# A decoder step with 32 experts: router turned round and woven into the last projection, samples turned ahead of the mask, weights fetched in the order of need from the fourth pair on

## What is computed

```python
def rms_norm(x, g):
    return x * lax.rsqrt(jnp.mean(x * x, axis=-1, keepdims=True) + EPS) * g

def decoder_layer(x, ...):
    y, ... = head_group_mixer(rms_norm(x, g_mix), ...)   # projections, RG-LRU scan, conformer conv
    x = x + y
    x = x + cross_attention(rms_norm(x, g_xa), mem_k, mem_v, w_q, w_o)
    x = x + routed_experts(rms_norm(x, g_moe), moe_w)
    return x, ...

def routed_experts(xf, ...):                      # N tokens x 1024
    logits = xf @ w_router + b_router             # 32 experts
    top_v, top_e = lax.top_k(logits, 4)
    gates = jax.nn.softmax(top_v, axis=-1)
    ...                                           # tokens sorted by expert
    gu = xb @ w_e1[e] + b_e1[e]                   # 1024 -> 2048
    g = jnp.minimum(gu[:, :1024], 7.0)
    u = jnp.clip(gu[:, 1024:], -7.0, 7.0)
    h = (u + 1.0) * (g * jax.nn.sigmoid(1.702 * g))
    rows = h @ w_e2[e] + b_e2[e]                  # 1024 -> 1024
    ...                                           # times gate, summed over the 4 experts of a token
```

## Time and profile before

| | us |
|---|---|
| median of 3 runs | 1257.3 |
| lowest, highest | 1255.49, 1258.81 |
| profiled execution | 1259.0 |
| its span in the trace | 1257.4 |
| PE busy | 1160.8 (92%) |
| DVE busy | 335.7 (27%) |
| ACT busy | 181.5 (14%) |
| first expert matmul | 312.96 |
| last weight byte read | 1223.7 |

### The profile page before, as it was taken

One profiled execution on the slowest core, in us unless ns is written; L12 is line 12 of the kernel. 1 busy time (PEld: TensorE's weight loads), 2 busy tenths in 40 slices (PEclk: granted clock), 3 DMA queues, 4 the chain that ended last, 5 costly groups with the idle time before them and its releaser, 6 DMA issues.

```text
span 1257.4 us, 14280 instructions
## 1 busy us (share of the span) xinstructions
PE 1160.8 (92%) x5512; PEld 567.2 (45%) x5512; DVE 335.7 (27%) x814; ACT 181.5 (14%) x353; POOL 45.6 (4%) x87
## 2 busy tenths in 40 slices
PE   8999999698999999989999898999898999999996
PEld 6887888387343343323333333334233333333332
DVE  3795423615112212021212121212212021212113
ACT  3114213203010110111010101010110111010102
POOL 4000001100000000000000000000000000000000
PEclk9999999798899999999999999999999999999998
DMA  9388434993899999999999999999999999999990
GB/s 301 95 285 283 138 101 135 342 424 126 343 429 427 428 427 428 426 429 428 427 427 429 428 427 429 427 428 427 430 427 427 428 428 428 427 429 428 427 397 35
DMA packets 65575, 457.42 MB, mean 364 GB/s; under 512 B 5491, under 2 KB 34379, under 8 KB 40837
## 3 DMA queue, kind: packets, MB, share of 16 engines
q1 hardware_dynamic: 62576, 452.00, 87.6%
q10 hardware_dynamic: 1117, 3.04, 0.6%
q0 software_dynamic: 1856, 2.02, 0.6%
HBM read 453.71 MB, written 3.81 MB: 364 GB/s over the span
## 4 chain that ended last, share of the span: by engine, by line
PE 54%; DMA 39%; DVE 4%; ACT 1%; issue 1%; ACTq 0%; SPq 0%; POOL 0%; DVEq 0%
DMA ring<-in_w_e 39%; PE ps L1589 21%; PE ps L1307 11%; PE ps L1608 8%; PE ps L1326 3%; PE ps L1556 2%; DVE ring L997 2%; PE ps L1565 2%; PE ps L1510 1%; PE ps L1469 1%; PE ps L1598 1%; PE ps L1254 1%; PE ps L1243 1%; PE ps L1501 1%; PE ps L1248 0%
## 5 line engine op out<-in xcount | busy, mean ns | idle before, releaser
L1589 PE MATMUL ps<-ring,mixed 128*64 128x512 f32 x1536 | 351.8, 607 | 50.4 <-DMA ring<-in_w_e 49.3
L1589 PEld LDWEIGHTS ps<-ring,mixed 128*64 128x64 f32 x1536 | 108.2, 139 | 278.6 <-issue 197.6
L1608 PE MATMUL ps<-ring,mixed 128*64 128x512 f32 x1024 | 230.9, 604 | 0.7 <-issue 0.7
L1147 DVE TENSOR_SCALAR mixed<-ps 128x512 f32<-128x512 f32 x32 | 22.1, 691 | 592.1 <-PE ps L1589 592.1
L1608 PEld LDWEIGHTS ps<-ring,mixed 128*64 128x64 f32 x1024 | 71.9, 139 | 157.9 <-issue 145.8
L721 ACT ACTIVATE mixed<-mixed 128x512 f32<-128x512 f32 x32 | 20.2, 630 | 530.0 <-DVE mixed L1147 530.0
L1565 PEld LDWEIGHTS ps<-mixed 128*128 128x128 f32 x512 | 64.1, 200 | 25.8 <-issue 24.3
L1565 PE MATMUL ps<-mixed 128*128 128x128 f32 x512 | 70.0, 292 | 1.3 <-ACT rstd L703 1.3
L731 ACT ACTIVATE mixed<-ps 64x512 f32<-64x512 f32 x64 | 37.8, 591 | 230.4 <-PE ps L1608 230.0
L1134 DVE SCALAR_TENSOR_TENSOR mixed<-mixed,gates 128x1024 f32<-128x1024 f32 x15 | 19.3, 1285 | 153.2 <-ACT mixed L731 153.2
L1307 PE MATMUL ps<-mixed,ring 128*128 128x264 f32 x256 | 58.9, 393 | 0.3 <-ACT mixed L674 0.3
(11 more groups left out here) (299 smaller groups left out, 775.8 us busy)
## 6 DMA issues: line engine op xcount, KB each, us to landing
ring<-in_w_e SPq DMA_DIRECT2D x160, 2048.0 KB, 23.6
low<-in_w_e SPq DMA_DIRECT2D x15, 2048.0 KB, 25.4
mixed<-in_w_e SPq DMA_DIRECT2D x15, 2048.0 KB, 26.7
ring<-in_w_in SPq DMA_DIRECT2D x8, 1024.0 KB, 15.6
ring<-in_cache_mem_k SPq DMA_DIRECT2D x8, 1024.0 KB, 4.8
ring<-in_cache_mem_v SPq DMA_DIRECT2D x8, 1024.0 KB, 8.3
ring<-in_w_k SPq DMA_DIRECT2D x4, 1024.0 KB, 8.9
ring<-in_w_v SPq DMA_DIRECT2D x4, 1024.0 KB, 12.6
```

What stands on the lines that cost most here:

```text
L1147: dve.tensor_scalar(g1, ps[0][:, :], LIMIT, None, ALU.min).then_inc(S["g_clamped"], 1)
L1589: m = pe.matmul(ps[gu][CAP * i:CAP * i + CAP, :], xeT[:, k, CAP * e2:CAP * e2 + CAP], w[:, D * gu + 512 * i:D * gu + 512 * i + 512], start ...
L1608: m = pe.matmul(ps[3][CAP * i:CAP * i + CAP, :], hTv[:, k % 4, CAP * (k // 4):CAP * (k // 4) + CAP], ring[:, s, D * (k % 2) + 512 * i:D * ...
```

## The change

**Router.** `turn_tokens` and the logits' matmuls go. `project` calls `between_tiles` after each output tile: `turn` transposes the tile before to banks 4 to 6 (three transposes), and `route` adds it to router sums in bank 7 with the operands exchanged, `wr[:, k, :]` stationary and the 264 tokens moving; the squares, made by ScalarE tile by tile, are summed in the same way with ones. Each takes 32 columns of the array, another four for odd k. After the last tile VectorE copies the sums, and three small matmuls with `spread` (two stacked identities and a column of 1/32) give logits and mean square by token. `xnt` now holds the raw tokens; 1/rms goes into the one-hot values and the gain into the copy of the gathered rows (`keep_gathered`: eight copies with scale instead of two; in the first pair VectorE does half of them). The tiles 0 and 1 go through logits and mask ahead of the samples' tile. The samples' own turning (L1664 before) becomes a matmul with a diagonal of 1/rms ahead of the mask, and the gates come after the first gather.

**First and last pair.** The output bias is added for both tiles in the first pair. Half of the samples' early matmuls (`early_samples`) moves from the last up projection to behind `turn_gates`.

**Weights.** From pair 4 (`EARLY_PAIRS`) on the order in SP's queue is rest of 2q, head of 2q+1, rest of 2q+1, head of 2q+2. The late half of `high` waits for `logit_done`.

```diff
-            def two_experts(q, last):
-
-                if last:
-                    rest(2 * q, 2 * q)
-                for s in range(0, HEAD_SLOTS, 2):
-                    fill(2 * q + 1, s, used(2 * q - 1, s + 1))
-                if not last:
-                    rest(2 * q, 2 * q)
-                    for s in range(0, HEAD_SLOTS, 2):
-                        refill(2 * q + 2, s, used(2 * q, s + 1))
+            with sp.Fori(1, EARLY_PAIRS) as q:
+                odd_half(q)
+                rest(2 * q, 2 * q)
+                even_half(q + 1)
                 rest(2 * q + 1, 2 * q + 1)
...
+            with sp.Fori(EARLY_PAIRS, PAIRS - 1) as q:
+                rest(2 * q, 2 * q)
+                odd_half(q)
+                rest(2 * q + 1, 2 * q + 1)
+                even_half(q + 1)
+            rest(NE - 2, NE - 2)
+            odd_half(PAIRS - 1)
+            rest(NE - 1, NE - 1)
...
-            pool.wait_ge(S["xnt_kept"], 6)
+            pool.wait_ge(S["logit_done"], 1)
             pool.memset(acc, 0.0).then_inc(S["acc_zeroed"], 1)
...
+            def turn(k):
+
+                pe.wait_ge(S["res_added"], KD + k + 1)
+                if k == 4:
+                    pe.wait_ge(S["tokr_kept"], 3)
+                for t, (t0, rows) in enumerate(TT):
+                    m = pe.transpose(ps[4 + t][0:rows, P * (k % 4):P * (k % 4) + P], xT[:, k, t0:t0 + rows], ident[:, :])
...
+            def route(k):
+
+                r = NE * (k % 2)
...
+                pe.matmul(ps[7][r:r + NE, 0:TOK], wr[:, k, :], xn[:, k, :], start=(k < 2), stop=(k >= KD - 2))
+                r += 2 * NE
+                m = pe.matmul(ps[7][r:r + NE, 0:TOK], ones[:, 0:NE], squares[:, k, :], start=(k < 2), stop=(k >= KD - 2))
...
+            project("o", "o_done", lambda k: oT[:, k, :], o_free, lambda k: None, after=between_tiles)
...
+            dve.tensor_copy(sums, ps[7][:, 0:TOK]).then_inc(S["sums_kept"], 1)
...
-                                                 rkp[:, t, bass.ds(col, 1)], None, ALU.is_equal)
+                                                 rkp[:, t, bass.ds(col, 1)], trs[:, t:t + 1], ALU.is_equal, ALU.mult)
...
                 if first:
+                    pe.wait_ge(S["gt0_kept"], 1)
                     pe.wait_ge(S["be2_loaded"], 16)
-                    rounds(None, 0)
-                if last:
-                    pe.wait_ge(S["acc_done"], 2 * q)
+                    for t in range(2):
+                        rounds(None, t, PAIR_BANKS[t])
...
                 turn_gates(q)
+                if last:
+                    early_samples(1)
                 turn_h(2 * q + 1)
```

More of the change, by code:

```diff
@@ L196, in build @@
         ysb = part(D)
+        acc = part(D)
         b1q = part(512)
-        acc = part(D)
+        sums = part(TOK)
+        diag = part(NB)
         assert pos[0] <= ATTENTION_W
@@ new lines, in _, with logits @@
+            wide = [P, 3, 4, NE]
+            def logits(tiles):
+                for t in tiles:
+                    rows = TT[t][1]
+                    dve.scalar_tensor_tensor(out=lg[0:rows, t, :], in0=root_of[0:rows, t, 0:NE], scalar=trs[0:rows, t:t + 1],
+                                             in1=brout[0:rows, :], op0=ALU.mult, op1=ALU.add).then_inc(S["lg_ready"], 1)
+                dve.wait_ge(S["lg_ready"], 2 if tiles[0] == 0 else 5)
+                for t in tiles:
+                    dve.max(m8[:, t, :], lg[:, t, :]).then_inc(S["lg_ready"], 1)
+                dve.wait_ge(S["lg_ready"], 4 if tiles[0] == 0 else 6)
@@ new lines, in _ @@
+            logits((0, 1))
+            chosen((0, 1), 0)
+            dve.wait_ge(S["eq_ready"], 1)
+            dve.tensor_reduce(mask[:, 0:2, :], eq[:, 0:2, :, :].rearrange("p t k e -> p t e k"), AX.X, ALU.add).then_inc(S["mask_ready"], 1)
+            logits((2,))
+            dve.tensor_scalar(nv0, m8[:, :, 0], -1.0, None, ALU.mult).then_inc(S["v0_ready"], 1)
+            dve.wait_ge(S["mask_ready"], 1)
+            dve.tensor_scalar(rk[:, 0:2, :], mask[:, 0:2, :], -BIG, BIG, ALU.mult, ALU.add).then_inc(S["rank_chain"], 1)
@@ new lines, in _, with one_hot @@
+            dve.wait_ge(S["rank_chain"], 1)
+            dve.wait_ge(S["rank_done"], 1)
+            dve.tensor_tensor(rkp[:, 0:2, 0:NE], rk[:, 0:2, :], ps[7][:, 0:2 * NE].rearrange("p (t e) -> p t e", t=2),
+                              ALU.add).then_inc(S["rank_chain"], 1)
+            dve.wait_ge(S["rank_chain"], 2)
+            def one_hot(cols):
+                for t in range(2):
+                    for i, col in enumerate(cols):
+                        last = dve.tensor_scalar(sel[:, t, CAP * i:CAP * i + CAP], iota_s[:, :],
+                                                 rkp[:, t, bass.ds(col, 1)], trs[:, t:t + 1], ALU.is_equal, ALU.mult)
+                last.then_inc(S["sel_ready"], 1)
@@ L1165, in _ @@
             swiglu(0)
-            add_round(0, 0)
+            for t in range(2):
+                add_round(0, t, PAIR_BANKS[t])
             next_pair(0, first=True)
@@ L1533, in _ @@
                     lhs = before if i == t else ones
-                    m = pe.matmul(ps[5][:, NE * t:NE * t + NE], lhs[:, :], mask[:, i, :], start=(i == 0), stop=(i == t))
+                    m = pe.matmul(ps[7][:, NE * t:NE * t + NE], lhs[:, :], mask[:, i, :], start=(i == 0), stop=(i == t))
             for i in range(2):
-                m = pe.matmul(ps[5][:, 96:128], ones[:, :], mask[:, i, :], start=(i == 0), stop=(i == 1))
+                m = pe.matmul(ps[7][:, 96:128], ones[:, :], mask[:, i, :], start=(i == 0), stop=(i == 1))
             m.then_inc(S["rank_done"], 1)
-            for j in range(10, 12):
-                turn_tokens(j)
-            pe.wait_ge(S["gate_chain"], 4)
-            for t, (t0, rows) in enumerate(TT):
-                m = pe.transpose(ps[4][0:NE, t0:t0 + rows], gcol[0:rows, t, :], ident[0:rows, 0:rows])
-            m.then_inc(S["gt0_turned"], 1)
             def rounds(q, t, bank=6):
@@ L1612, in down, with early_samples @@
                         m.then_inc(S["freed"], 1)
+            def early_samples(i):
+                cols = slice(512 * i, 512 * i + 512)
+                pe.matmul(ps[LAST_BANKS[2] + i][0:NB, :], gateT[:, SEQ:TOK], be2[0:NE, cols], start=True, stop=False)
+                pe.matmul(ps[LAST_BANKS[2] + i][0:NB, :], pick8[:, :], acc[:, cols], start=False, stop=False)
             def pair(q, first=False, last=False):
@@ L1618, in gather_next @@
                     if k == 3 and not last:
[L1619 to L1620 removed]
+                        pe.wait_ge(S["acc_done"], 2 * q + 2)
                         gather(q + 1, (0,))
```

253 lines of the change are left out of this document (128 added, 125 removed).

## The result

| | before | after |
|---|---|---|
| median, us | 1257.96 (6 runs, 1255.49 to 1259.51) | 1249.45 (6 runs, 1247.85 to 1250.25) |
| profiled execution / its span | 1259.0 / 1257.4 | 1250.25 / 1248.7 |
| start of the output projection | 258.81 | 257.47 |
| end of its last tile | 289.03 | 294.26 |
| first expert matmul | 312.96 | 314.25 |

The ratio is 0.9932, 95% interval 0.9919 to 0.9945: 0.7% faster, 8.5 us, where 16 were forecast. The spans differ by 8.7 us, and the table splits that into three: the experts start 1.3 us later, the stream of weights loses 0.7 us more in the first pair (2.9 for 2.2), and the stretch from the last byte to the end of the last down is 8.5 us instead of 19.2, 10.7 less. So the tail came as forecast, and router and first pair, forecast at -3.1 and -2.0, cost 2.0 us together.

What follows compares the result with a forecast made beforehand. Expert weight transfers at 427 GB/s were taken as the bound. Tail -10.9, first pair -2.0 and router -3.1 sum to -16.0 us, from 1257.3 to 1241.3, stated as 1241.5; the 8-in-10 range was 1237 to 1250.

Steps and rivals of the forecast that it cites:

- Order and tail: End of the kernel: transfers in order of need let the last down projection end earlier, at full clock; -10.9 us.
- rival 4: Expert stream: short waits at nearly every transfer lower TensorE's clock and slow the kernel, 1281 us; chance 0.05.
- rival 1: First pair and tail: TensorE's clock falls at both short holes, giving 1246.7 us; chance 0.15.
- last 14.5 us unchanged: Sign that the forecast holds: the kernel's last 14.5 us stay as they were.
- Rival 3: Tail: it is TensorE's own work and does not shrink with the transfer order; 1246.3 us, chance 0.09.
- First pair: First expert pair: with no idle time left the weight stream no longer runs short; -2.0 us.
- The bound +0.8: First pair: value if the clock falls to 1.2 GHz there too and the longer rounds add time.
- Router ahead of the last tile: Output projection: six turns and six router steps between tiles, 0.80 us each, add +4.8 us, bound +7.4.
- The prediction's sign of being wrong: Output projection: tiles over 4.7 us apart would show the forecast wrong.
- Router behind the last tile: Last projection tile to first expert matmul: 15.6 us instead of 23.9, -8.3 us, bounds -9.6 and -6.9.
- Clearing beside the copy: Router: GpSimd's clearing of the sums' rows blocks VectorE's copy of the sums; +0.4 us.
- rival 2: Router: steps run one by one and the chain behind is slower, router +0.9, 1245.3 us; chance 0.14.

Runs made afterwards that it cites:

- run 1: Changed kernel with the transfers of pairs 4 to 14 put back into the old order; 1252.98 us, ratio 0.9958.
- run 2: Kernel before with only the new order of transfers from pair 4 on; 1251.53 us, ratio 0.9953.
- run 3: Changed kernel with the new order of transfers from the first pair of the loop instead of the fourth; 1256.62 us, ratio 0.9994.
- run 4: Changed kernel with the first pair's bias rounds given 128 rows, 96 of them zeros; 1247.03 us, ratio 0.9916.
- run 9: Changed kernel with router steps taken two at a time behind every second tile, the last two behind the last tile; 1245.85 us, ratio 0.9903.
- run 8: Changed kernel with all eight router steps behind the last projection tile; 1244.70 us, ratio 0.9892.
- run 5: Changed kernel with useless matmuls filling TensorE's holes in the router and the up bias behind the small matmuls; 1251.2 us, ratio 0.9938.
- run 6: Changed kernel with useless matmuls in the router's holes and first-pair bias rounds of 128 rows, 96 of them zeros; 1246.87 us, ratio 0.9915.
- run 10: Changed kernel with all router steps behind the last tile and first-pair bias rounds of 128 rows, 96 of them zeros; 1243.49 us, ratio 0.9880.
- run 11: Kernel of run 10 with useless matmuls only at TensorE's standstills and in the samples' diagonal, up bias behind the ranks; 1246.17 us, ratio 0.9904.
- run 7: Kernel before, with its own router, plus the new transfer order and the first- and last-pair changes; 1248.10 us, ratio 0.9920.

## Why the prediction was right, and where it was wrong

**Order and tail: right** (-10.9 forecast, -10.7 by the traces). The steps hold one by one: in step with the transfers by the last expert, hole 0.63 us, down 7.09 us, no fall of the clock at the short holes (rival 4 falls, and rival 1 for the tail), last 14.5 us unchanged (14.5 and 14.6). Runs 1 and 2 show what the sum did not say, that order and last-pair edits each give more than half of it and overlap: the old order with the new last pair has 12 to 13 us behind the last byte, and the new order with the old last pair 11 to 12, of which it pays 2.5 us for the clock behind its hole. Rival 3 fell with run 2. Run 3 bears out that the first pairs have no stock to spend.

**First pair: wrong** (-2.0 forecast, +0.7 measured). The step that failed is "I take -2.0, for there is no idle time left between up projection and transposes". It took idle time as what the clock fell after. The trace after has none and the clock fell (0.85 in 328.20:334.42, then 0.74); run 4 keeps the same busy time, fills the rows with zeros, and it stays up, as it does in the four other kernels with padded rounds. The bound +0.8, written beside it for this case, was the value.

**Router ahead of the last tile: mis-sized** (+4.8 forecast, +6.6 measured; that the last tile ended at 294.26 where 293.8 was forecast is the earlier start of the projection, not a hit). The term is 6 x 0.80 with 0.36 for a turn and 0.44 for a step. A turn cost 3.89 - 3.56 = 0.33; a step cost 0.76. I had costed the step by its passes, two column groups at a time, and not the break in the stream of tiles: the first pass starts 0.10 us later behind the turn than a tile does (0.42 for 0.32), the second 0.25 behind the first, the second holds the engine 0.32 us until the tile, and the tile behind it takes 3.83 instead of 3.73, which makes the 0.76. And since 32 of the bank's rows alternate between even and odd steps, taking them one at a time left half of the width unused, which run 9 shows. The prediction's sign of being wrong, tiles over 4.7 us apart, was too lax: 4.65 us stayed under it and still cost 1.8 us more than the sum had.

**Router behind the last tile: mis-sized** (-8.3 forecast, -3.9 measured; 15.6 us forecast, 20.0 measured). To the logits it took 4.75 us instead of 4.1; 0.4 of it because the small matmuls waited behind the up bias (296.29 to 297.31) when the sums were already copied (296.91). Logits to mask took 2.46 for 2.4: right. Mask to one-hots took 3.9 for 1.8: the samples' diagonal, said to lie "beside the ranks and the gather", stood in front of the ranks until 302.65 while the mask was there at 301.47, and the ranks took 2.35 us at 1.2 GHz. One-hots to gather took 1.1 for 0.7, the gather 6.48 for 5.45, and the step to the experts 1.3 for 1.1. Most of the 4.4 us is the clock, an estimate from these rows: at full clock the diagonal takes 2.05 us (run 8) and would end before the mask, 1.2 us; the ranks take 1.2 (run 5), 1.1 us less; the gather 1.0 over its forecast; 3.3 together. I took the old gather's mean of 0.71 over into a chain with three rows of small, half-empty matmuls before it. And 1.2 of the 4.4 us is this one execution, since runs 1 and 3 took 18.8 us with the same code.

**Clearing beside the copy: wrong** (+0.4 forecast, 0 measured). The copy of the sums took 0.43 us beside GpSimd's clearing, no more than a residual of the same size:

```profile
296.48 0.43 DVE L1056 COPY mixed<-ps 128x264 f32<-128x264 f32 x1 [1.20 <-PE ps L1560]
```

```profile
296.44 0.95 POOL L516 MEMSET mixed<- 128x1024 f32 x1 [43.71 <-PE ps L1560]
```

The rule of the Trainium skill ("SBUF — State Buffer", section "Who interferes with whom") that the prediction set against its row held: no contention for one input from PSUM. Its other half, that `tensor_scalar` can use both ports and then blocks or is blocked whole, agrees with runs 4, 6, 10 and 11: 1.70 us instead of 0.98.

So of rival 2 ("the router only moves") the direction was right and its bound, +0.9, too mild: the router cost 2.6 us in the trace, and 1.35 by the medians of run 7. The range held the time because it took that rival in, and in part by luck: 1249.45 lies 0.55 us inside its upper end of 1250, where neither the forecast (1241.5, its own range ending at 1246) nor any of rivals 1 to 3 (1245.3 to 1246.7) stood. Only the tail was foreseen as it came.

## What to carry to other kernels

A small step woven into a stream of large matmuls costs its passes and the break it makes, whatever the room beside it: gather such steps until they fill all column groups, or put them behind. When a chain of small operations is shortened, look at the clock it will run at; busy time in the rows does not say that the clock stays up, and filling a hole pays only where the filler ends before the wait does. A gain in a tail has two parts, when the last data comes and what is left to do at which clock, and each can hide the other. Rest no stage on one trace where the clock may fall at another moment: look at a second run with the same code there.

## What the runs showed of the hardware

- TensorE's clock fell from 2.4 to 1.2 GHz with no idle time in the rows: in the first pair (1.00 until 328.20) after 3.7 us of matmuls on 32 rows, and in run 11 right after 8.8 us of mixed small work that had run at 1.00. With zeros in the 96 missing rows it did not fall, at the same busy time, in five kernels of five. No run tried data in their place.
- The moment of the fall differs between executions of the same code (the diagonal took 3.58, 3.15 and 3.23 us in the changed kernel and runs 1 and 3, 2.05 in run 8). What sets it stays open.
- Passes of 264 columns start 0.22 us apart at full clock, whether one fills all 128 columns of the array (3.56 us for the 16 of a tile) or four of 32 columns run side by side (run 8).
- One-hots by `tensor_scalar` in SBUF beside GpSimd clearings of 0.94 and 0.95 us took 0.72 us longer; a copy out of PSUM beside one of 0.95 took no longer.
